# Modulation rows in four column groups, gate rows behind the first projection, and q/k/v transposes issued inside the following job

## The chip, the core and the metric

The kernel runs on one core of a Trainium2 chip. The metric is the device time in microseconds (us) of one execution. TensorE (PE) multiplies, its weight loads have a row of their own (PEld); VectorE (DVE), ScalarE (ACT) and GpSimd (POOL) do elementwise work; SyncE's queue (SP) issues most transfers.

## The reference, cut to what matters

Two layers. Each modulates the stream `u = h * (1 + scale) + shift`, projects it, and lets three mixers read it; attention needs all of q, k and v.

```
shift, scale, gate = split(silu(c) @ w_mod[l] + b_mod[l], 3)       # 1024 -> 3 x 1024, latent
shift_c, scale_c, gate_c = the same from c_ctx                      # context tokens
u_lat = h_lat * (1 + scale) + shift;  u_ctx = h_ctx * (1 + scale_c) + shift_c
p = u @ w_in[l]                                                     # q, k, v, gates, conv inputs
q = rope(rms_norm(q, q_gain)); k = rope(rms_norm(k, k_gain))        # 8 query heads, 2 kv heads, 64 wide
o = attention(q, [k_ctx; k_lat], [v_ctx; v_lat]); merge of three branches; @ w_out
h = layer_norm(alpha * h + gate * out)
```

1024 latent and 256 context tokens; in the last layer the context tokens give only k and v.

## The kernel before

Features lie on the partitions: a projection **job** computes 128 output features for all tokens T (1280 in layer 0, 1024 for most of layer 1) into one of two PSUM slots. Its weights are split by POOL into a high and a low part (`wh`, `wl`, lines 493 and 495), the input likewise (`Uh`, `Ul`), and for each of 8 blocks k of the contraction the job issues three products, `wh*Uh`, `wl*Uh`, `wh*Ul` (line 608). Job 0 of each layer is special: since `Uh` and `Ul` are still being made, it first does all products with `Uh`, waiting per block, and then all with `Ul` (line 613).

**Modulation.** `csilu` holds silu(c) and silu(c_ctx), 2 columns for each of 8 blocks. `mod_rows` (line 640) multiplies it with 512 columns of `w_mod` at a time: an output of 2 partitions x 512. Layer 0 takes the 2048 shift and scale columns from the tiles `wmA`, 8 tiles of 1 MB and four products each, and the 1024 gate columns from `wmB`, 8 tiles of 0.5 MB and two products each; layer 1 takes all six products of a block from `wmL`. DVE copies the rows out (`mod_row`, line 1163), PE transposes them into columns in pieces of 128 (`mod_cols`, line 648), and DVE adds the bias (`mod_col`, lines 1168 and 1173). Then `make_u` (ACT lines 891 and 895, DVE lines 1188 and 1193) makes `Uh` and `Ul` from blocks of h. In layer 0 these blocks are loaded in pairs into two buffers: SP's order is wmA, the first pair, the weights of jobs 0 and 1, all of wmB, and then the other three pairs, each block as soon as the one before it in its buffer was read (line 426). The rope tables land where wmB was, so their loads wait until the gate rows are done, and POOL's tables (line 515) wait for them. In layer 1 the rows of `wmL` are interleaved with the two LayerNorm statistics of layer 0's end (`stat`, line 633): block 0, the mean, blocks 1 to 4, the variance, blocks 5 to 7.

**q, k and v.** Jobs 0 to 5 are K, Q0, Q1, Q2, Q3 and V. After each, ACT copies the slot to one of two buffers `fc` (`evac`, line 912), PE transposes it to token-major form (line 626) in pieces of at most 4 x 128 tokens, alternating between two PSUM banks, and ACT copies each piece to one of two `raw` buffers (line 920) and squares it (line 934). DVE sums the squares (`mean_square`, 1208), POOL takes the power -0.5 (`rms`, 523), and DVE normalises, multiplies by the rope tables and adds (`normed`, lines 1215 to 1240). The normalised keys are transposed back (`to_keys`, operations KT0 and KT1), ACT copies them and DVE takes the low part (line 1247). V needs a copy and a low part on DVE (lines 956 and 1264). On DVE the order is K, Q0, Q1, KT0, KT1, Q2, Q3, V, each a mean square and a norm. Attention starts on PE with line 712, and before it all of these must be there.

PE's order in both layers is: job 0, job 1, K transposes, job 2, Q0 transposes, job 3, Q1 and KT0, job 4, KT1, Q2 and Q3, job 5, V, attention.

Of the kernel before, what the change touches and what calls it, by code (L numbers as in the profile page):

```python
# [17 lines left out]
F32 = mybir.dt.float32  # L18
F32R = mybir.dt.float32r
ACT = mybir.ActivationFunctionType  # L20
# [166 lines left out]
def build(nc, hT_in, cvec, wmod, w8, w4, vecs, gains, rope, ident_in, stack_in, outT):  # L187
    with ExitStack() as ctx:
# [11 lines left out]
        def at(name, shape, dt, offset):  # L200
            return nc.alloc_sbuf_tensor_at(name, shape, dt, offset=offset)
# [23 lines left out]
        modrow = [at("modrow0", [2, 3 * D], F32, rY), at("modrow1", [2, 3 * D], F32, rU + 5 * 12288)]  # L225
# [44 lines left out]
        csilu = small("csilu", [P, KD, 2])  # L270
# [96 lines left out]
        def jobs_qkv(l):  # L367

            return [TALL] + [TL[l]] * 4 + [TALL]
# [112 lines left out]
        def _(pool):  # L482
# [20 lines left out]

            nc.gpsimd.memset(ones[:], 1.0 / D).then_inc(s_ones, 1)
            nc.gpsimd.memset(mhalf[:], -0.5).then_inc(s_ones, 1)
            nc.gpsimd.memset(eps[:], LN_EPS).then_inc(s_ones, 1)
            pool.wait_ge(s_ones, 3)
# [85 lines left out]
        def _(pe):  # L593
# [27 lines left out]
            def transposes(l, op, srcs):  # L621

                for f, c, n in pieces(l, op):
# [20 lines left out]
            def mod_cols(l, first, n, at_col, turn):  # L644

                pe.wait_ge(s_modrow, turn)
                for m in range(first, first + n):
                    last = nc.tensor.transpose(PS[:, at_col + 2 * m:at_col + 2 * m + 2],
                                               modrow[l][0:2, m * P:(m + 1) * P], ident[0:2, 0:2])
                last.then_inc(s_modtr, 1)  # L650

            pe.wait_ge(s_csilu, 1)
            for k in range(KD):
                mod_rows(k, wmA, 0, 2 * D, s_wm[k], 16)
            mod_cols(0, 0, 2 * KD, 3072, 1)
            for k in range(KD):
                mod_rows(k, wmB, 2 * D, D, s_wmb, 16 * KD)

            for l in range(DEPTH):
# [5 lines left out]
                def qkv_job(n):  # L665
                    job((jl + n) // 2, n % 2, KD, jobs_qkv(l)[n], Uh, Ul,
                        (lambda k: pe.wait_ge(s_ufp, KD * l + k + 1)) if n == 0 else None,
                        (lambda k: pe.wait_ge(s_u, KD * l + k + 1)) if n == 0 else None)

                def to_tokens(f, n):  # L670
                    pe.wait_ge(s_fc, 6 * l + n + 1)
                    transposes(l, f, [fc[n % 2][:, t * P:(t + 1) * P] for t in range(jobs_qkv(l)[n] // P)])

                def to_keys(f, g):
                    pe.wait_ge(s_kd, l + 1)
                    transposes(l, f, [kd[:, t, g].rearrange("p a d -> p (a d)") for t in range(NTOK)])
# [180 lines left out]
                if nxt:  # L857
                    for p in range(2):
                        pe.wait_ge(sfree[p], (jl + NJ) // 2)
                    mod_rows(0, wmL, 0, 3 * D, s_wm[0], 32)  # L860
                pe.wait_ge(s_csum, 4 * l + 3)
                stat(l, O_OMEAN, e[4])
                if nxt:
                    for k in range(1, 5):
                        mod_rows(k, wmL, 0, 3 * D, s_wm[k], 32)
                pe.wait_ge(s_csum, 4 * l + 4)
                stat(l, O_OVAR, e[5])
                if nxt:
                    for k in range(5, KD):
                        mod_rows(k, wmL, 0, 3 * D, s_wm[k], 32)  # L870
                    mod_cols(l + 1, 0, 3 * KD, 0, 3)
# [3 lines left out]
        def _(act):  # L875
# [3 lines left out]
            fn(csilu[:], craw[:], ACT.Silu).then_inc(s_csilu, 1)  # L879
# [21 lines left out]
            for l in range(DEPTH):  # L901
# [45 lines left out]
                if l > 0:  # L947
                    act.wait_ge(s_hst, 16 * KD)
                k_hi(O_KT0, 0)
                evac(4)  # L950
                k_hi(O_KT1, 1)
                square(O_Q2)
                square(O_Q3)
                evac(5)
# [201 lines left out]
        def _(dve):  # L1156
# [4 lines left out]
            def mod_row(l, c0, n, turn):  # L1161
# [3 lines left out]
            def mod_col(l, first, n, at_col, turn):  # L1165
                dve.wait_ge(s_modtr, turn)
                cols = PS[:, at_col + 2 * first:at_col + 2 * (first + n)].rearrange("p (n w) -> p n w", w=2)
                last = tt(mod[:, l, first:first + n], cols,
                          vec[:, l, V_BM + first:V_BM + first + n].rearrange("p (n w) -> p n w", w=1)
                          .broadcast_to([P, n, 2]), ALU.add)  # L1170
                if first == 0:
                    st.done(last)
                    last = ts(mod[:, l, KD:2 * KD], mod[:, l, KD:2 * KD], 1.0, None, ALU.add)
                last.then_inc(s_mod, 1)

            mod_row(0, 0, 2 * D, 1)
            mod_col(0, 0, 2 * KD, 3072, 1)

# [17 lines left out]
            mod_row(0, 2 * D, D, 2)  # L1196
            mod_col(0, 2 * KD, KD, 3072, 2)

            for l in range(DEPTH):
# [305 lines left out]
                for j in range(KD):  # L1505
                    if l + 1 < DEPTH and j == KD // 2:
                        mod_row(l + 1, 0, 3 * D, 3)
                    tt(Z[:, j, :T], Z[:, j, :T], e[4][:, :T], ALU.mult).then_inc(s_norm, 1)
                if l + 1 < DEPTH:
                    mod_col(l + 1, 0, 3 * KD, 0, 3)  # L1510
                    make_u(l + 1, lambda j: X[:, j, :], lambda j: dve.wait_ge(s_hn, KD * l + j + 1))
# [69 lines left out]
```

## Time and profile before

| | us |
|---|---|
| median of 3 runs | 2991.51 |
| the three runs | 2988.11, 3004.97, 2991.51 |
| span of the profiled execution | 2990.4 |
| PE busy in it | 2783.8 (93%) |
| PEld busy | 2230.2 (75%) |
| DVE / POOL / ACT busy | 1472.9 / 876.1 / 819.5 |

The page gives no own time of the profiled execution beside its span; the median of the runs is 1.1 us above the span. PE is busy nearly everywhere. What it isn't lies in a few places, among them the first 75 us, the q/k/v stretch of either layer, and the passage from layer 0 to layer 1 at about 1600 to 1680 us.

### The profile page before, as it was taken

The numbers are of one execution on the slowest core, as the hardware profiler recorded it, in microseconds if no ns is written. First come the engines' busy times: TensorE is split into PE (matmuls) and PEld (weight loads), VectorE is DVE, ScalarE is ACT, GpSimd is POOL, SyncE is SP. The second block draws the span as 40 slices with busy tenths as digits, with TensorE's granted clock in tenths as the row PEclk, the third lists the DMA queues.
The fourth block names the chain that finished last, engine by engine and source line by source line (L and its number), as shares of the span: only waits on it lengthen the run. The fifth ranks groups of instructions, "written<-read, shape, count | busy, mean of one in ns | idle before, by whom it ended". The sixth has DMA issues, their size and how long they took to land.

```text
span 2990.4 us, 35900 instructions
## 1 busy us (share of the span) xinstructions
PE 2783.8 (93%) x13592; PEld 2230.2 (75%) x13592; DVE 1472.9 (49%) x1428; ACT 819.5 (27%) x1334; POOL 876.1 (29%) x818
## 2 busy tenths in 40 slices
PE   8889997999999999989999779999999999999994
PEld 3767776788888888878884557777888888877872
DVE  2577773216742168731225567775136323862135
ACT  2357673200001110120112447775100111012013
POOL 1610000223333233323232440000444434543340
PEclk9989997999999999999999889999999999999996
DMA  7100000011211113212233300000112111321221
GB/s 292 36 8 0 0 0 1 29 39 50 77 60 35 42 59 105 90 43 65 79 143 129 120 29 1 0 0 7 43 49 85 63 49 48 118 84 60 98 78 63
DMA packets 47033, 177.70 MB, mean 59 GB/s; under 512 B 5472, under 2 KB 5728, under 8 KB 44896
## 3 DMA queue, kind: packets, MB, share of 16 engines
q1 hardware_dynamic: 37728, 138.74, 13.6%
q10 hardware_dynamic: 9216, 37.75, 3.6%
q8 instruction: 59, 0.97, 0.1%
q14 instruction: 30, 0.25, 0.0%
HBM read 148.16 MB, written 28.31 MB: 59 GB/s over the span
## 4 chain that ended last, share of the span: by engine, by line
PE 79%; DVE 7%; ACT 6%; issue 5%; SPq 1%; POOL 1%; DMA 1%; DVEq 0%; ACTq 0%; POOLq 0%
PE PS L608 65%; PE PS L770 4%; PE PS L734 3%; PE PS L746 2%; DVE PTl L1313 1%; ACT Pr L978 1%; ACT Pr L982 1%; PE PS L640 1%; PE PS L757 1%; DVE nm L1286 1%; PE PS L712 1%; DVE e L1467 1%; DVE Ul L1489 1%; PE PS L633 1%; DMA wmB<-wmod 1%
## 5 line engine op out<-in xcount | busy, mean ns | idle before, releaser
L608 PE MATMUL PS<-Uh,wh 128*128 128x512 f32 x2816 | 773.6, 372 | 13.9 <-ACT Uh L895 12.3
L608 PE MATMUL PS<-Uh,wl 128*128 128x512 f32 x2816 | 769.7, 371 | 0.0
L608 PE MATMUL PS<-Ul,wh 128*128 128x512 f32 (+1 forms) x2728 | 744.7, 370 | 0.0
L493 POOL CAST wh<-wraw 128x512 fp32r<-128x512 f32 (+1 forms) x376 | 293.7, 781 | 1424.5 <-PE PS L608 963.6
L608 PEld LDWEIGHTS PS<-Uh,wh 128*128 128x128 f32 x2816 | 490.8, 189 | 113.1 <-issue 12.5
L608 PEld LDWEIGHTS PS<-Uh,wl 128*128 128x128 f32 x2816 | 490.9, 189 | 97.4
L608 PEld LDWEIGHTS PS<-Ul,wh 128*128 128x128 f32 x2728 | 474.5, 188 | 94.2
L495 POOL TENSOR_TENSOR wl<-wraw,wh 128x512 fp32r<-128x512 f32 (+1 forms) x376 | 510.0, 1356 | 30.1
L1372 DVE SCALAR_TENSOR_TENSOR cv<-hc,vec,cv x360 | 394.4, 1123 | 49.7 <-DVE cv L1372 38.0
L1054 ACT ACTIVATE e<-PS 128x1280 f32<-128x1280 f32 (+1 forms) x48 | 54.5, 1135 | 754.8 <-PE PS L608 754.7
L1313 DVE TENSOR_TENSOR PTl<-PS,PTh 128x512 fp32r<-128x512 f32 x328 | 211.1, 684 | 55.5 <-ACT PTh L996 48.1
L1286 DVE TENSOR_REDUCE nm<-PS 128x1 f32<-128x1280 f32 (+1 forms) x144 | 196.8, 1372 | 62.3 <-PE PS L734 53.5
L770 PE MATMUL PS<-ident,Pr 128*128 128x128 f32 x1312 | 187.5, 284 | 41.1 <-DVEq L1304 12.9
L996 ACT ACTIVATE PTh<-PS 128x512 fp32r<-128x512 f32 x328 | 183.6, 602 | 133.8 <-PE PS L770 133.3
L770 PEld LDWEIGHTS PS<-ident,Pr 128*128 128x128 f32 x1312 | 145.6, 143 | 77.4 <-DVE PTl L1313 33.6
L734 PE MATMUL PS<-kT,qTh 128*128 128x512 f32 (+1 forms) x400 | 167.3, 418 | 14.6 <-ACT Pr L978 7.7
L553 POOL COPY qd<-qo 128x512 f32 (+1 forms) x36 | 22.0, 616 | 536.9 <-PE PS L734 532.5
L734 PE MATMUL PS<-kT,qTl 128*128 128x512 f32 (+1 forms) x400 | 148.6, 372 | 0.0
L608 PE MATMUL PS<-Yh,wh 128*128 128x512 f32 (+1 forms) x480 | 133.0, 374 | 13.5 <-DVE Yl L1482 13.5
L982 ACT ACTIVATE Pr<-PS,nm 128x1024 f32<-128x1024 f32 x128 | 142.9, 1117 | 0.0
L1400 DVE SCALAR_TENSOR_TENSOR e<-PS,vec,e 128x1280 f32<-128x1280 f32 (+1 forms) x16 | 22.7, 1418 | 234.9 <-PE PS L608 234.9
L746 PE MATMUL PS<-PTh,Vt 128*128 128x512 f32 x328 | 137.2, 418 | 0.0
(135 smaller groups left out, 2525.2 us busy)
## 6 DMA issues: line engine op xcount, KB each, us to landing
wraw<-w SPq DMA_DIRECT2D x140, 512.0 KB, 3.5
wraw<-w SPq DMA_DIRECT2D x48, 256.0 KB, 2.7
wmL<-wmod SPq DMA_DIRECT2D x8, 1536.0 KB, 12.0
e<-hT_in SPq DMA_DIRECT2D x16, 640.0 KB, 4.7
accd<-e ACTq DMA_DIRECT2D x16, 640.0 KB, 3.2
e<-accd ACTq DMA_DIRECT2D x16, 640.0 KB, 4.0
wmA<-wmod SPq DMA_DIRECT2D x8, 1024.0 KB, 12.2
accd<-e ACTq DMA_DIRECT2D x16, 512.0 KB, 3.0
```

The source lines that it names most:

```text
L493: nc.gpsimd.tensor_copy(wh[par][:, s], wraw[par][:, s]).then_inc(whi[par], 1)
L495: nc.gpsimd.tensor_tensor(wl[par][:, s], wraw[par][:, s], wh[par][:, s].bitcast(F32), ALU.subtract).then_inc(wsplit[par], 1)
L608: last = mmul(PS[:, SLOT[par] + c:SLOT[par] + c + n], w[par][:, k * P:(k + 1) * P], x[:, k, c:c + n], start=(k == 0 and a == 0), stop=(k = ...
L734: last = mmul(PS[:, s0 + c:s0 + c + n], x[g][:, h * P:(h + 1) * P], kT[:, g, k0 * P + c:k0 * P + c + n], start=(a == 0), stop=(a == 1))
L746: last = mmul(PS[:, O0:O0 + 512], Vt[:, k0 + kt, g, :], x[b][:], start=(kt == 0 and a == 0), stop=(kt == nk - 1 and a == 1))
L770: last = nc.tensor.transpose(PS[:, PT0[par] + h * P:PT0[par] + (h + 1) * P], Pr[:, g, h, kt * P:(kt + 1) * P], ident[:])
L982: fn(Pr[:, g, h, c:c + 1024], PS[:, s0 + c:s0 + c + 1024], ACT.Exp, bias=nm[:, m:m + 1], accum_out=rs[:, g, 1, h:h + 1]).then_inc(s_exp, 1)
L996: fn(PTh[pt_buf(g, kt)][:], PS[:, PT0[par]:PT0[par] + 512], ACT.Copy).then_inc(pt_hi[par], 1)
L1054: fn(e[0][:, :T], slot(0, T), ACT.Sigmoid).then_inc(sfree[0], 1)
L1286: nc.vector.reduce_max(nm[:, m:m + 1], PS[:, s0:s0 + nk * P], AX_X, negate=True).then_inc(s_nm, 1)
L1313: tt(PTl[b][:], PS[:, PT0[par]:PT0[par] + 512], PTh[b][:].bitcast(F32), ALU.subtract).then_inc(pt_free[par], 1)
L1372: last = stt(cv[:, i + c_base, c0:c0 + n], hc[:, i + c_base, CPAD * who + c0 + tap:CPAD * who + c0 + tap + n], vec[:, l, bass.ds(i * CONF_ ...
```

## The change

Three things are changed.

1. `csilu` gets 32 columns for each block, 2 real ones and 30 zeros (a memset on POOL, for which ACT waits once at the start), and a product of `mod_rows` writes 32 partitions x 512, at partition 32q for the q-th 512 columns: four column groups of the array and one PSUM bank for shift and scale, two groups and another bank for the gate. The number of products stays 32 + 16 + 48. DVE's copy becomes 128 x 512 (64 x 512 for the gate), PE's transposes 4 of 128 partitions (4 of 64) in place of 16 (8) of 2 partitions, and the bias is added through a strided view.
2. In layer 0 the 16 gate products run behind job 0 and not ahead of it, and their 4 transposes inside job 2.
3. The K, Q0 and Q1 transposes run inside jobs 2, 3 and 4 (a piece ahead of some block k of the contraction), KT0 and KT1 inside job 5, and Q2, Q3 and V behind job 5. On ACT `evac(4)` comes ahead of KT0, and `evac(5)` ahead of the square of Q3. DVE, POOL and SP keep their order.

```diff
-            def mod_rows(k, w, col0, ncol, landed, n):
+            def mod_rows(k, w, parts, landed, n):
 
                 pe.wait_ge(landed, n)
-                for n in range(ncol // 512):
-                    last = mmul(PS[0:2, col0 + n * 512:col0 + (n + 1) * 512], csilu[:, k, :],
-                                w[k][:, n * 512:(n + 1) * 512], start=(k == 0), stop=(k == KD - 1))
+                for col0, ncol, bank in parts:
+                    for q in range(ncol // 512):
+                        last = mmul(PS[32 * q:32 * q + 32, bank:bank + 512], csilu[:, k, :],
+                                    w[k][:, col0 + q * 512:col0 + (q + 1) * 512], start=(k == 0), stop=(k == KD - 1))
                 last.then_inc(s_wmu, 1)
...
             for k in range(KD):
-                mod_rows(k, wmA, 0, 2 * D, s_wm[k], 16)
-            mod_cols(0, 0, 2 * KD, 3072, 1)
-            for k in range(KD):
-                mod_rows(k, wmB, 2 * D, D, s_wmb, 16 * KD)
+                mod_rows(k, wmA, [(0, 2 * D, 0)], s_wm[k], 16)
+            mod_cols(0, [(0, P, 3072)], 1)
...
+                def in_job2(k):
+                    if l == 0 and k == 1:
+                        mod_cols(0, [(1, 64, 3072)], 2)
+                    if l == 0 and k == 2:
+                        pe.wait_ge(s_mod, 2)
+                    if k in (3, 4, 6):
+                        to_tokens(O_K, 0, (3, 4, 6).index(k))
+
+                def in_job34(f, n):
+                    def hook(k):
+                        if k in (2, 3, 5):
+                            to_tokens(f, n, (2, 3, 5).index(k))
+                    return hook
+
+                def in_job5(k):
+                    if 1 <= k < 4:
+                        to_keys(O_KT0, 0, k - 1)
+                    if 4 <= k < 7:
+                        to_keys(O_KT1, 1, k - 4)
 
                 qkv_job(0)
                 if l == 0:
-                    pe.wait_ge(s_mod, 1)
-                    mod_cols(0, 2 * KD, KD, 3072, 2)
-                    pe.wait_ge(s_mod, 2)
+                    for k in range(KD):
+                        mod_rows(k, wmB, [(0, D, 3584)], s_wmb, 16 * KD)
                 qkv_job(1)
-                to_tokens(O_K, 0)
-                qkv_job(2)
-                to_tokens(O_Q0, 1)
-                qkv_job(3)
-                to_tokens(O_Q1, 2)
-                to_keys(O_KT0, 0)
-                qkv_job(4)
-                to_keys(O_KT1, 1)
+                qkv_job(2, in_job2)
+                qkv_job(3, in_job34(O_Q0, 1))
+                qkv_job(4, in_job34(O_Q1, 2))
+                qkv_job(5, in_job5)
                 to_tokens(O_Q2, 3)
                 to_tokens(O_Q3, 4)
-                qkv_job(5)
                 to_tokens(O_V, 5)
...
-                nc.vector.tensor_copy(modrow[l][:, c0:c0 + n], PS[0:2, c0:c0 + n]).then_inc(s_modrow, 1)
+                for part, rows, bank in parts:
+                    last = nc.vector.tensor_copy(modrow[l][0:rows, part, :], PS[0:rows, bank:bank + 512])
+                last.then_inc(s_modrow, 1)
```

At the kernel's start PE has this order before (`modrow` are the modulation rows; the first job's rows start with `Uh`):

```order
L640 MATMUL PS<-wmA_80,csilu 2x512 x4
L648 MATMUL PS<-ident,modrow_63 128x2 x16
L640 MATMUL PS<-wmB_81,csilu 2x512 x2
...
L640 MATMUL PS<-wmB_88,csilu 2x512 x2
L608 MATMUL PS<-Uh,wh_121 128x512 x2
```

And this one after:

```order
L644 MATMUL PS<-wmA_80,csilu 32x512 x4
L653 MATMUL PS<-ident,modrow_63 128x128 x4
L609 MATMUL PS<-Uh,wh_121 128x512 x2
...
L614 MATMUL PS<-Ul,wh_121 128x256
L644 MATMUL PS<-wmB_81,csilu 32x512 x2
...
L644 MATMUL PS<-wmB_88,csilu 32x512 x2
L609 MATMUL PS<-Uh,wh_122 128x512 x2
```

The gate rows have moved from ahead of job 0 (weights `wh_121`) to between it and job 1 (`wh_122`), and every product is 32 partitions high.

Around job 5 of layer 0 PE has this before (`kd` are the normalised keys, `fc_58` and `fc_57` the two feature copies, `qd` the first operand of attention):

```order
L608 MATMUL PS<-Ul,wh_121 128x256
L626 MATMUL PS<-ident,kd 128x128 x10
L626 MATMUL PS<-ident,fc_58 128x128 x10
L626 MATMUL PS<-ident,fc_57 128x128 x10
L608 MATMUL PS<-Uh,wh_122 128x512 x2
...
L626 MATMUL PS<-ident,fc_58 128x128 x10
L712 MATMUL PS<-ident,qd_108 128x128 x4
```

And this after:

```order
L609 MATMUL PS<-Ul,wh_122 128x256
L629 MATMUL PS<-ident,kd 128x128 x2
L609 MATMUL PS<-Uh,wh_122 128x512 x2
...
L609 MATMUL PS<-Ul,wh_122 128x256
L629 MATMUL PS<-ident,fc_58 128x128 x10
L629 MATMUL PS<-ident,fc_57 128x128 x10
L629 MATMUL PS<-ident,fc_58 128x128 x10
L732 MATMUL PS<-ident,qd_108 128x128 x4
```

The key transposes have moved into job 5, and those of Q2 and Q3 from ahead of job 5 to behind it, where only V's stood.

## Rows read from the trace of the kernel before

**Rows 1.** Stretches of time: stretch, length, busy us (instructions) per engine, PE clock, DMA, GB/s

```profile
30.00:35.00 5.00, 5.00 (x13) 0.97 (x12) 0.00 (x0) 0.00 (x0) 4.76 (x6) 1.00 1.03 415
40.00:45.00 5.00, 4.66 (x19) 1.34 (x19) 2.18 (x5) 3.71 (x4) 0.00 (x0) 0.70 0.19 50
```

**Rows 2.** Timeline, 8 to 78 us: start, us, engine, line, operation [idle before, releaser]

```profile
8.03 29.24 PE L640 MATMUL PS<-wmA,csilu 128*2 128x512 f32 x64 [8.03 <-DMA wmA<-wmod]
...
29.77 0.61 POOL L493 CAST wh<-wraw 128x512 fp32r<-128x512 f32 x1 [28.73 <-DMA wraw<-w]
...
37.31 2.28 DVE L1163 COPY modrow<-PS 2x2048 f32<-2x2048 f32 x1 [37.31 <-PE PS L640]
...
41.13 15.59 PE L640 MATMUL PS<-wmB,csilu 128*2 128x512 f32 x32 [0.34 <-DMA wmB<-wmod]
41.26 1.73 ACT L891 ACTIVATE e<-e,mod 128x1024 f32<-128x1024 f32 x2 [36.29 <-DVE mod L1173]
...
46.79 1.73 ACT L891 ACTIVATE e<-e,mod 128x1024 f32<-128x1024 f32 x2 [1.34 <-DMA e<-hT_in]
...
62.16 1.28 ACT L895 ACTIVATE Uh<-e 128x1280 fp32r<-128x1280 f32 x1 [1.13 <-DVE e L1188]
...
66.08 4.83 PE L613 MATMUL PS<-Ul,wh 128*128 128x512 f32 x24
...
71.35 2.94 POOL L515 TENSOR_TENSOR e<-cosT,gain 128x1280 f32<-128x1280 f32 x1 [33.93 <-DMA gain<-gains]
...
77.14 0.61 POOL L493 CAST wh<-wraw 128x512 fp32r<-128x512 f32 x1
```

**Rows 3.** Chain of waits, in order of time: start, us, what

```profile
71.75 14.29 PE PS L608 x72
...
145.79 13.78 PE PS L608 x72
...
1684.88 11.16 PE PS L608 x48
```

**Rows 4.** Timeline, q/k/v of layer 0, columns as in rows 2

```profile
140.52 1.07 PE L626 MATMUL PS<-ident,fc 128*128 128x128 f32 x8
...
161.06 2.44 DVE L1240 TENSOR_TENSOR qo<-qa,qb 128x1280 f32<-128x1280 f32 x1
...
164.52 2.15 DVE L1264 TENSOR_TENSOR Vt<-raw,Vt 128x1280 fp32r<-128x1280 f32 x1 [1.01 <-ACT Vt L956]
...
167.75 1.94 PE L712 MATMUL PS<-ident,qd 128*128 128x128 f32 x8 [4.98 <-POOL qd L553]
```

**Rows 5.** Timeline, from layer 0 to layer 1, columns as in rows 2

```profile
1598.24 5.31 PE L640 MATMUL PS<-wmL,csilu 128*2 128x512 f32 x12 [1.62 <-issue]
...
1600.10 1.78 DVE L1502 TENSOR_TENSOR e<-e,Z 128x1280 f32<-128x1280 f32 x1
...
1603.48 2.51 PE L633 MATMUL PS<-e,ones 128*128 128x512 f32 x6
...
1633.08 15.61 PE L640 MATMUL PS<-wmL,csilu 128*2 128x512 f32 x36
...
1642.04 5.70 DVE L1508 TENSOR_TENSOR Z<-Z,e 128x1280 f32<-128x1280 f32 x4
...
1648.73 3.35 DVE L1163 COPY modrow<-PS 2x3072 f32<-2x3072 f32 x1 [0.99 <-PE PS L640]
```

**Rows 6.** Timeline, job 0 and q/k/v of layer 1, columns as in rows 2

```profile
1662.38 1.40 PE L608 MATMUL PS<-Uh,wh 128*128 128x512 f32 x3 [8.22 <-ACT Uh L895]
...
1698.81 1.27 ACT L934 ACTIVATE sq<-raw 128x1280 f32<-128x1280 f32 x1
...
1763.40 1.22 DVE L1240 TENSOR_TENSOR qo<-qa,qb 128x1024 f32<-128x1024 f32 x1
...
1769.42 1.49 DVE L1264 TENSOR_TENSOR Vt<-raw,Vt 128x1280 fp32r<-128x1280 f32 x1 [4.80 <-ACT Vt L956]
...
1772.09 1.94 PE L712 MATMUL PS<-ident,qd 128*128 128x128 f32 x8 [4.43 <-POOL qd L553]
```

More of the change, by code:

```diff
@@ L269, in build @@
         craw = small("craw", [P, KD, 2])
-        csilu = small("csilu", [P, KD, 2])
+        csilu = small("csilu", [P, KD, 32])
         mod = small("mod", [P, DEPTH, 3 * KD, 2])
@@ L502, in split_merge @@
                         split(i * 4 + (jb // 2 + j), 1, W3)
+            nc.gpsimd.memset(csilu[:], 0.0).then_inc(s_ones, 1)
             nc.gpsimd.memset(ones[:], 1.0 / D).then_inc(s_ones, 1)
@@ L506, in _ @@
             nc.gpsimd.memset(eps[:], LN_EPS).then_inc(s_ones, 1)
[L507 removed]
+            pool.wait_ge(s_ones, 4)
             for l in range(DEPTH):
@@ L619, in piece_wait, with transposes @@
                     pe.wait_ge(t_free, f - 1)
-            def transposes(l, op, srcs):
-                for f, c, n in pieces(l, op):
+            def transposes(l, op, srcs, which=None):
+                for i, (f, c, n) in enumerate(pieces(l, op)):
+                    if which is not None and which != i:
+                        continue
                     piece_wait(f)
@@ L633, in stat, with mod_cols @@
                     mmul(tbank(f, n), ones[:], src[:, c:c + n], start=True, stop=True).then_inc(t_done, 1)
-            def mod_rows(k, w, col0, ncol, landed, n):
+            def mod_rows(k, w, parts, landed, n):
                 pe.wait_ge(landed, n)
-                for n in range(ncol // 512):
-                    last = mmul(PS[0:2, col0 + n * 512:col0 + (n + 1) * 512], csilu[:, k, :],
-                                w[k][:, n * 512:(n + 1) * 512], start=(k == 0), stop=(k == KD - 1))
+                for col0, ncol, bank in parts:
+                    for q in range(ncol // 512):
+                        last = mmul(PS[32 * q:32 * q + 32, bank:bank + 512], csilu[:, k, :],
+                                    w[k][:, col0 + q * 512:col0 + (q + 1) * 512], start=(k == 0), stop=(k == KD - 1))
                 last.then_inc(s_wmu, 1)
-            def mod_cols(l, first, n, at_col, turn):
+            def mod_cols(l, parts, turn):
                 pe.wait_ge(s_modrow, turn)
-                for m in range(first, first + n):
-                    last = nc.tensor.transpose(PS[:, at_col + 2 * m:at_col + 2 * m + 2],
-                                               modrow[l][0:2, m * P:(m + 1) * P], ident[0:2, 0:2])
+                for part, rows, at_col in parts:
+                    for m in range(4):
+                        last = nc.tensor.transpose(PS[:, at_col + m * rows:at_col + (m + 1) * rows],
+                                                   modrow[l][0:rows, part, m * P:(m + 1) * P], ident[0:rows, 0:rows])
                 last.then_inc(s_modtr, 1)
@@ L671, in to_tokens, with to_keys @@
+                def to_tokens(f, n, which=None):
                     pe.wait_ge(s_fc, 6 * l + n + 1)
-                    transposes(l, f, [fc[n % 2][:, t * P:(t + 1) * P] for t in range(jobs_qkv(l)[n] // P)])
-                def to_keys(f, g):
+                    transposes(l, f, [fc[n % 2][:, t * P:(t + 1) * P] for t in range(jobs_qkv(l)[n] // P)], which)
+                def to_keys(f, g, which=None):
                     pe.wait_ge(s_kd, l + 1)
-                    transposes(l, f, [kd[:, t, g].rearrange("p a d -> p (a d)") for t in range(NTOK)])
+                    transposes(l, f, [kd[:, t, g].rearrange("p a d -> p (a d)") for t in range(NTOK)], which)
@@ L878, in _ @@
             act.wait_ge(s_c, 64)
-            fn(csilu[:], craw[:], ACT.Silu).then_inc(s_csilu, 1)
+            act.wait_ge(s_ones, 4)
+            fn(csilu[:, :, 0:2], craw[:], ACT.Silu).then_inc(s_csilu, 1)
             def make_u(l, src):
@@ L1158, in _, with mod_row, mod_col @@
             tt, stt, ts = nc.vector.tensor_tensor, nc.vector.scalar_tensor_tensor, nc.vector.tensor_scalar
-            def mod_row(l, c0, n, turn):
+            def mod_row(l, parts, turn):
                 dve.wait_ge(s_wmu, KD * turn)
-                nc.vector.tensor_copy(modrow[l][:, c0:c0 + n], PS[0:2, c0:c0 + n]).then_inc(s_modrow, 1)
-            def mod_col(l, first, n, at_col, turn):
+                for part, rows, bank in parts:
+                    last = nc.vector.tensor_copy(modrow[l][0:rows, part, :], PS[0:rows, bank:bank + 512])
+                last.then_inc(s_modrow, 1)
+            def mod_col(l, parts, turn):
                 dve.wait_ge(s_modtr, turn)
[L1167 to L1173, printed above, removed]
+                for part, rows, at_col in parts:
+                    nq, first = rows // 32, 2 * KD * part
+                    cols = PS[:, at_col:at_col + 4 * rows].rearrange("p (m q w) -> p q m w", m=4, q=nq, w=32)
+                    last = tt(mod[:, l, first:first + 4 * nq].rearrange("p (q m) w -> p q m w", m=4),
+                              cols[:, :, :, 0:2],
+                              vec[:, l, V_BM + first:V_BM + first + 4 * nq].rearrange("p (q m w) -> p q m w", m=4, w=1)
+                              .broadcast_to([P, nq, 4, 2]), ALU.add)
+                    if part == 0:
+                        st.done(last)
+                        last = ts(mod[:, l, KD:2 * KD], mod[:, l, KD:2 * KD], 1.0, None, ALU.add)
                 last.then_inc(s_mod, 1)
-            mod_row(0, 0, 2 * D, 1)
-            mod_col(0, 0, 2 * KD, 3072, 1)
+            mod_row(0, [(0, P, 0)], 1)
+            mod_col(0, [(0, P, 3072)], 1)
             def make_u(l, src, landed):
```

34 lines of the change are left out of this document (18 added, 16 removed).

## The prediction

> **What bounds the kernel now.** I read the page first: PE is busy 93% of the span and its products are the chain nearly everywhere, so the three edits can only change stretches in which PE waits, or does work that they shorten. I then read the stretches by timeline and chain. There are four: the start up to job 1, q/k/v of layer 0, the passage to layer 1, and q/k/v of layer 1. In each the reader is to see which wait ends last.
>
> At the start the rows of wmA hold PE from 8.03 to 37.27 [rows 2]: 64 records of 0.43 us on average, two for each of 32 products, one behind the other. But the transfers are saturated too, 415 GB/s [rows 1], in the order in which SP issued them: the first job's weights are used at 29.77, and wmB lands at 41.13 [rows 2], though it was issued long before. Then `make_u` runs from 41.26, and its second pair starts only at 46.79, since its block was issued when the first was read (41.26 + 1.73 = 43.0) and took 3.8 us. A pair takes 5.6 us, and the last `Uh` ends at 63.44. PE does the gate rows meanwhile (41.13 to 56.72) and then job 0, and job 1 starts at 71.75 [rows 2, 3]. So the gate rows are free today: they lie under `make_u`.
>
> In q/k/v of layer 0 PE stands for some us between jobs, and from job 5's end at 159.57 to 167.75 ahead of attention [rows 3, 4]. There V's copy, transposes and low part (DVE, 164.52 to 166.67) come last; the norms of Q2 and Q3 had job 5 as cover and ended at 163.50 [rows 4]. In layer 1 V's low part is last again (1770.91), but DVE's norm of Q3 ended at 1764.62, with DVE idle for 4.8 us in between [rows 6].
>
> **The start.** With several column groups at work a block of wmA takes less time on PE than its 1 MB takes to land (1.05 MB at 0.42 MB/us is 2.5 us; PE needs 29.24 / 8 = 3.66 us today). The transfers set the end: from the first weights at 29.77 I go back by 0.52 MB of weights and 1.31 MB of the first pair, 4.4 us, so the last wmA tile is there at about 25.4. Then products 0.9 to 2.2, copy 0.6 (2.28 for 2048 columns [rows 2], now 512), transposes 0.6, bias 0.4, latencies: the modulation stands at about 29 in place of 41.2. That looks like 12 us. But the second pair lies in SP's queue behind wmB, which lands at 41.1 as before. It lands at about 42.5, so of 12 us the chain of `make_u` keeps 46.79 - 42.5 = 4.3. The last `Uh` ends at 59.1. Job 0 follows it: one block, 1.2 us at full clock or 2.3 at half (the first in layer 1 took 1.40 for three of its six products after a pause [rows 6]), then the `Ul` products, 4.83 [rows 2]. PE will have stood long before, and the granted clock falls after pauses (0.70 of full in 40 to 45 us [rows 1], between levels of 1.2 and 2.4 GHz). I take 66.5, between 65.1 and 71. Now the gate rows, which were free, stand in the path: 16 products, 15.59 us one by one [rows 2]. Of two column groups I expect half: 7. Job 1 starts at 73.6, **1.9 us later than before**. The rope loads wait for the gate rows: POOL's tables started 6.3 us behind the last `Ul` (63.44 + 1.5, against 71.35) and need 5.8, and the first half of job 2's weights 2 more [rows 2], so 73.5 + 14.1, against job 1's end at 73.6 + 14.3 [rows 3]. No stall, with no margin; a miss costs 1 or 2 us.
>
> The copy width, the csilu memset (0.3 us on idle POOL) and DVE's wait for the gate transposes in job 2 (nothing is queued behind it until the first squares) I put at nothing.
>
> **The trace against the Trainium skill.** The rows show that two columns of weights stream no faster than 128, and that nothing ran side by side; no row shows column groups. The Trainium skill (TensorE: Matmul & The Clock Gate, Part 3: Packing small matmuls) reports 2.38 times for three column tiles of 32 with 512 columns. It also says that matmuls start in program order; with two records for each fp32 product on one group, this would allow one product per 0.43 us, not four at once. By that the gate rows are 6.9 us too and the rest of my sum stands, since transfers bound wmA. The page on DMA: Bandwidth & Descriptors (Queues, rings and completion order) has descriptors consumed in ring order, which agrees with 29.77 against 41.13 above; no run here shows the contrary.
>
> **q/k/v of layer 0.** Removed are PE's pauses at the edges of jobs 2 to 5: from job 1's end at 86.04 [rows 3] to attention are 81.7 us, in which four jobs take 13.8 to 13.9 each, and 8.2 are the end, so 18 go into the edges. In their place stand the transposes, 50 of 0.13 us (1.07 for 8 [rows 4]), in the jobs, 6.5, and 4 gate transposes, 0.5. Job 5 then ends 62.5 us behind job 1 in place of 73.5: 11 gained. But behind it now stands all of Q2, Q3 and V. From the first Q2 transpose to the end of Q3's norm are 140.52 to 163.50, 23.0 us [rows 4], of which about 0.5 was ACT being busy with KT1, so 22.5; then V's low part, which is behind it on DVE, 1.5 to 2.15 (1.6), and 1.1 from there to PE (166.67 to 167.75). That makes 25.2 in place of 8.2: 17 lost. **Sum +6.0.** The K squares come about 9 us later, which moves POOL's tables and the norms; they still end just ahead of job 5's end, and job 4's weights about 1 us ahead of its start. This is tight: +0 to +3, and if ACT's `evac(5)` ahead of Q3 costs its 1.25 once more, +1.
>
> **The passage.** Block 0's six products take 5.31 and hold the mean's product until 1603.48, though its sum was ready at 1600.10 + 1.78 = 1601.9 [rows 5]. Shorter by half or more they end before it: -1.5. The variance waits for DVE. Blocks 5 to 7, 15.6 us, end at 1648.7, and DVE, done with four Z at 1647.74, waits 1.0 for them, then copies 3.35 [rows 5]. Half the products, even at half clock to begin with, end before that, and two copies of 512 take 1.3: -1.0 - 2.05. **Sum -4.5**, all on the chain into `make_u`.
>
> **q/k/v of layer 1.** The DVE chain decides. K's squares start 2.8 us behind job 1's end (1684.88 + 11.16 = 1696.04) [rows 3, 6]; with its last piece ahead of block 6 of job 2 (6 x 1.39 + 1.3 of transposes and copies) it is 10.2, so 7.5 later. From there DVE and POOL went without waiting for PE up to the norm of Q3, ended 1764.62; now 1772.1. V's low part, 1.5, and 1.2 to PE [rows 6]: 1774.8 against 1772.09. **+2.8** (-1 to +6, for POOL and DVE slow each other when they meet: a copy of 1280 on DVE takes 1.49 alone, 2.15 and more then).
>
> **Sum.** +1.9 + 6.0 - 4.5 + 2.8 = +6.2. On the span of 2990.4 that is 2996.6; the median stood 1.1 above it, so 2997.7, rounded 2998.
>
> **Rivals.**
> - **The column groups do not overlap**, the case that ends slower. For it: nothing in the trace shows them working at once. Then wmA ends at 37.3 as before and only the copy is shorter (-1.5); job 0 ends at 69.0, the gate rows take 15.6 in the path, and job 1 starts at 84.7, +12.9. With +6.0, with -2.0 at the passage (the copy alone) and +2.8: **+19.7, 3011.** It decides where two groups take over some 12 us for the gate rows.
> - **The second pair overtakes wmB.** Then it lands 3.8 us after its issue at 31, job 0 ends at about 58.5, and job 1 starts at 65.6: -6.1 + 6.0 - 4.5 + 2.8 = **-1.8, 2990.** Against it: the order of landing above.
> - **The norm chain is no limit**, so that attention starts as soon behind job 5 as in layer 0 before, 8.2 us. Layer 0 then gains 11, layer 1 I put at 11.5, its edges costing as much: 1.9 - 11 - 4.5 - 11.5 = **-25, 2966.** This is what hiding transposes would bring if PE's pauses were all. Against it: Q2's and Q3's norms take the same 23 us wherever they start, and only job 5 covered them.
> - **A cold clock through job 0 and the gate rows**: +4.5 for `Ul` and +3 to 5 for the rows, **3006.**
>
> **How the numbers follow.** My forecast 0.60, no overlap 0.18, overtaking 0.09, cold clock 0.08, no limit 0.05. The forecast's own range is 2990 to 3005. The range from 2988 to 3012 takes in all but the fourth and some of no overlap. A measurement of this kernel can tell about 0.5%, 15 us, from no change. Faster by more than that is the -25 case, 0.05; slower (over 3006.5) is no overlap and part of the cold clock, 0.21; the same 0.74.
>
> **What the profile after would show.** Right: the first `Uh` at about 31, a pause on PE until about 43 behind two blocks, the second pair at 42.5; gate rows of about 7 us between jobs 0 and 1; no pauses inside jobs 2 to 5; 25 us between job 5 and line 732's transposes in layer 0 and some 22 in layer 1, with DVE busy; the mean's product at about 2 us after the last sum; DVE's modulation copy at once behind the fourth Z. Wrong: gate rows of 15 us, a second pair before 40, or attention within 15 us of job 5.

## The result, and the profile after

The changed kernel takes 3014.32 us (median of 20 runs, 2997.37 to 3017.21), the kernel before 3002.81 (20 runs, 2988.11 to 3008.1): a ratio of **1.0033, 95% interval 1.0019 to 1.0048**. The change costs about 10 us (5.7 to 14.4). The profiled execution of the changed kernel has a span of 3009.2, the one of before 2990.4, and of these 18.8 us only some 11 are the change's. The rest is told under the fourth experiment. A difference of a third of a per cent is small, so what the change does is read from the stages of the traces, and the ratios only say whether they add up.

The start of the changed kernel, by timeline (start, us, engine, line, operation [idle before, releaser]):

```profile
25.24 1.06 PE L644 MATMUL PS<-wmA,csilu 128*32 128x512 f32 x8 [0.74 <-DMA wmA<-wmod]
26.38 0.69 DVE L1185 COPY modrow<-PS 128x512 f32<-128x512 f32 x1 [26.38 <-PE PS L644]
...
28.25 1.73 ACT L912 ACTIVATE e<-e,mod 128x1024 f32<-128x1024 f32 x2 [23.30 <-DVE mod L1199]
...
42.53 1.73 ACT L912 ACTIVATE e<-e,mod 128x1024 f32<-128x1024 f32 x2 [10.09 <-DMA e<-hT_in]
...
58.22 1.27 ACT L916 ACTIVATE Uh<-e 128x1280 fp32r<-128x1280 f32 x1 [1.11 <-DVE e L1214]
...
60.81 4.83 PE L614 MATMUL PS<-Ul,wh 128*128 128x512 f32 x24
...
65.57 7.06 PE L644 MATMUL PS<-wmB,csilu 128*32 128x512 f32 x32
...
72.56 0.85 PE L609 MATMUL PS<-Uh,wh 128*128 128x512 f32 x3
```

Read against [rows 2]: the column groups work at once. The last four products of wmA take 1.06 us where four took 29.24 / 8 = 3.66, and the 16 gate products 7.06 where they took 15.59. The modulation stands at 28.25 in place of 41.26. Of these 13 us the second pair of h gives back all but 4.3 (42.53 against 46.79), since ACT waits 10.09 us for it, and the gate rows take back more than the rest: job 1 starts at 72.56, 0.8 later than before.

The stretch ahead of attention in layer 0, by the same view:

```profile
137.89 3.53 POOL L524 TENSOR_TENSOR rstd<-ms,mhalf 128x20 f32<-128x20 f32 x1 [3.90 <-DVE ms L1235]
...
148.36 0.74 PE L609 MATMUL PS<-Ul,wh 128*128 128x512 f32 x3
...
148.94 1.04 PE L629 MATMUL PS<-ident,fc 128*128 128x128 f32 x8
...
151.94 1.51 ACT L941 ACTIVATE raw<-PS 128x512 f32<-128x512 f32 x3 [4.61 <-DVEq L1274]
...
152.10 1.49 DVE L1273 TENSOR_TENSOR kT<-raw,kT 64x1280 fp32r<-64x1280 f32 x1 [0.24 <-DVE kT L1273]
...
178.00 1.94 PE L732 MATMUL PS<-ident,qd 128*128 128x128 f32 x8 [14.39 <-POOL qd L554]
```

Job 5 ends at about 148.9, where before it ended at 159.57 [rows 3]. The pauses between jobs are gone. But attention starts at 178.00 against 167.75 [rows 4], and PE stands 14.39 us ahead of it in place of 4.98. From the last K transposes on, the chain up to there has nothing of PE in it but two short groups of transposes (0.45 us at 152.59, 0.70 at 156.71); it goes over POOL and DVE:

```profile
99.05 0.23 PE PS L629 x2
99.31 0.39 ACT raw L941
...
99.72 1.28 ACT sq L955
...
101.03 1.50 DVE ss L1234
...
106.31 7.11 POOL e L516 x2
...
137.89 3.54 POOL rstd L524
...
175.52 1.42 DVE Vt L1290
...
178.00 1.95 PE PS L732 x8
```

Later the passage to layer 1 (timeline):

```profile
1619.64 1.78 DVE L1528 TENSOR_TENSOR e<-e,Z 128x1280 f32<-128x1280 f32 x1
1621.53 2.51 PE L636 MATMUL PS<-e,ones 128*128 128x512 f32 x6 [1.85 <-DVEq L1529]
...
1666.11 1.27 DVE L1185 COPY modrow<-PS 128x512 f32<-128x512 f32 x2
...
1674.51 1.73 ACT L912 ACTIVATE e<-X,mod 128x1024 f32<-128x1024 f32 x2
...
1698.69 1.24 ACT L933 ACTIVATE fc<-PS 128x1280 f32<-128x1280 f32 x1 [6.20 <-PE PS L614]
...
1719.73 1.27 ACT L955 ACTIVATE sq<-raw 128x1280 f32<-128x1280 f32 x1
...
1791.63 1.94 PE L732 MATMUL PS<-ident,qd 128*128 128x128 f32 x8 [12.49 <-POOL qd L554]
```

The mean's product waits for DVE now and no longer stands behind block 0's rows [rows 5], and the copy of the rows takes 1.27, not 3.35. From line 1528 (1619.64) to `make_u` (1674.51) are 54.87 us. Attention in layer 1 starts 117.12 us behind `make_u`, and PE waits 12.49 us for it where it waited 4.43 [rows 6]. The row at 1698.69 is the end of job 0 in this layer; the account of the prediction comes back to it.

### The profile page after: what moved, and what is told of

Same layout as the page of the kernel before. It is cut to its first block, busy times and chain, and to the rows that moved or that the text cites. A ratio compares the mean times of both kernels' runs of the same rounds, so it can differ in the third digit from the quotient of the medians.

```text
span 3009.2 us, 35856 instructions
## 1 busy us (share of the span) xinstructions
PE 2743.8 (91%) x13560; PEld 2224.3 (74%) x13560; DVE 1474.1 (49%) x1430; ACT 820.3 (27%) x1334; POOL 883.0 (29%) x819
## 4 chain that ended last, share of the span: by engine, by line
PE 75%; DVE 9%; issue 6%; ACT 6%; POOL 2%; DMA 2%; DVEq 0%; SPq 0%; ACTq 0%; POOLq 0%
PE PS L609 62%; PE PS L790 4%; PE PS L754 3%; PE PS L766 2%; DVE PTl L1339 1%; ACT Pr L999 1%; ACT Pr L1003 1%; PE PS L777 1%; DVE nm L1312 1%; DMA e<-hT_in 1%; PE PS L732 1%; DVE e L1493 1%; DVE Ul L1515 1%; POOL wl L495 1%; POOL rstd L524 1%
## 5 line engine op out<-in xcount | busy, mean ns | idle before, releaser
L754 PE MATMUL PS<-kT,qTh 128*128 128x512 f32 (+1 forms) x400 | 165.3, 414 | 15.6 <-ACT Pr L999 8.5
```

Of the source, the lines that this page charges most:

```text
L754: last = mmul(PS[:, s0 + c:s0 + c + n], x[g][:, h * P:(h + 1) * P], kT[:, g, k0 * P + c:k0 * P + c + n], start=(a == 0), stop=(a == 1))
```

## The experiments

All ratios are to the kernel before, on the same chip. Diffs are against the changed kernel, and in them a minus is what the changed kernel has.

### The column groups alone

The gate rows go back ahead of job 0, and all transposes (those of the gate rows too, between jobs 0 and 1) and `evac` back to their old places.

```diff
+            for k in range(KD):
+                mod_rows(k, wmB, [(0, D, 3584)], s_wmb, 16 * KD)
...
-                qkv_job(2, in_job2)
-                qkv_job(3, in_job34(O_Q0, 1))
...
+                to_tokens(O_K, 0)
+                qkv_job(2)
+                to_tokens(O_Q0, 1)
+                qkv_job(3)
```

> The column groups alone: modulation rows as in the changed kernel, but the gate rows ahead of job 0 and all q/k/v transposes between the jobs as before. My theory (groups help, the two moves hurt): the gate rows run at about 41 to 48 us under the making of u, job 0 ends at about 65.6 and job 1 starts at about 66.5, 5 us earlier than before; the passage to layer 1 is 4 us shorter; in all 9 us faster than before, ratio 0.997. Rival (the groups are worth nothing because transfers or DVE set these stretches anyway): within 2 us of before.

Measured: 2993.65 us, ratio **0.9973 (0.9954 to 0.9992)**. Job 1 starts at 66.47, 5.3 earlier than before, and attention in layer 0 at 164.09, 3.7 earlier. The first part of the change gains 8 us (2 to 14). By stages it is 3.7 up to attention in layer 0, 4.8 in the passage (54.32 against 59.10) and 2.0 in q/k/v of layer 1 (110.94 from `make_u` to attention, against 112.89). What loses must be in the other two.

### The moved transposes alone

The narrow rows and the old place of the gate rows, with the third part of the change kept.

```diff
-                        last = mmul(PS[32 * q:32 * q + 32, bank:bank + 512], csilu[:, k, :],
+                    last = mmul(PS[0:2, col0 + n * 512:col0 + (n + 1) * 512], csilu[:, k, :],
...
+                    mod_cols(0, 2 * KD, KD, 3072, 2)
```

> The moved q/k/v transposes alone (part 3 of the change) on the kernel before. My theory: +6 to +9 us in q/k/v of layer 0 and +3 to +5 us in that of layer 1, with 23 to 26 us between job 5 and attention in layer 0; in all 10 to 13 us slower, ratio 1.004. Rival (the loss lies in the gate rows behind job 0 and not here): within 3 us of before.

Measured: 3015.78 us, ratio **1.0039 (1.0026 to 1.0053)**, about 12 us lost. Its start is that of before (job 1 at 71.71 against 71.75), and attention starts at 175.94, 8.2 later. In layer 1 attention stands 118.62 us behind `make_u` where before it stood 112.89, 5.7 later, which is more than the 3 to 5 expected. The whole loss of the third part is in these two stretches, with nothing of the modulation in it; the passage is 1.5 shorter in this profile.

### The gate rows ahead of job 0

```diff
+            for k in range(KD):
+                mod_rows(k, wmB, [(0, D, 3584)], s_wmb, 16 * KD)
...
-                if l == 0:
-                    for k in range(KD):
-                        mod_rows(k, wmB, [(0, D, 3584)], s_wmb, 16 * KD)
```

> The changed kernel with part 2 undone: the gate rows run ahead of job 0 again, their transposes still inside job 2. My theory: job 1 starts at about 65.6 us in place of 72.6, everything behind it 7 us earlier, so 7 us faster than the changed kernel and some 3 us slower than before. Rival (the rope tables' loads, which wait for the gate rows, or the clock set job 1's start): no more than 2 us faster than the changed kernel.

Measured: 3004.12 us, ratio **0.9998 (0.9982 to 1.0013)**, about 10 us below the changed kernel (the two intervals leave 2 to 20). Job 1 starts at 64.93 in place of 72.56, and attention in layer 0 at 169.85 in place of 178.00. By the trace it is thus about 8 us, close to the 7 expected. The second part of the change is a loss by itself. With the gate rows behind job 0, PE waits 9.34 us under `make_u` (to 45.62). Here they start when wmB lands, run from 41.10 to 49.86, and job 0 has made up for it by its last block, for which PE waits 0.30 us at 58.82. Behind job 0 PE has no such wait.

### The kernel before once more

> The kernel before once more, for a second profile of it. The changed kernel's products in the loops of layer 0 took 1.2% longer each than in the first profile of before (682.2 against 674.4 us for the same 3528), in code that the change does not touch. If that varies from execution to execution, this profile may show either figure, and its span either about 2990 or about 3003; if it belongs to the change, this profile shows 674 us again and 2990.

Measured: 3000.42 us, ratio 0.9996 (0.9976 to 1.0016). The longest piece in each chain (start, us, what), of before, of before once more, of the changed kernel and of the last experiment below:

```profile
580.31 674.37 PE PS L608 x3528
```

```profile
577.37 686.12 PE PS L608 x3528
```

```profile
590.27 682.21 PE PS L609 x3528
```

```profile
572.65 674.38 PE PS L609 x3528
```

The same instructions in the same program take 674.37 in one execution and 686.12 in another. So the 7.84 us by which the changed kernel's profile is longer here are not the change's: 18.8 - 7.8 leaves 11.0, inside the 5.7 to 14.4 of the ratio. Whether this stretch is also the main reason why runs of before lie between 2988 and 3008 us is not shown. The second profile of before spans 2994.7, only 4.3 more than the first, though it lost 11.75 us here: attention in layer 0 up to this stretch took it 407.7 us in place of 412.6 (169.67 to 577.37, against 167.75 to 580.31), and other parts vary by a us or two. The expectation named a span of about 2990 or about 3003, and neither came.

### The h pairs issued ahead of wmB

In the changed kernel's SP order four tiles of wmB follow the second pair of h, and four the third.

```diff
-                            for k in range(KD):
-                                sp.dma_start(wmB[k][:], wmod[0, k][:, 2 * D:]).then_inc(s_wmb, 16)
...
+                        if j in (3, 5):
+                            for k in range(2 * (j - 3), 2 * (j - 3) + 4):
+                                sp.dma_start(wmB[k][:], wmod[0, k][:, 2 * D:]).then_inc(s_wmb, 16)
```

> The changed kernel with one change in SP's queue: the second and third pair of blocks of h are issued ahead of the first and second half of wmB. My theory (the second pair waits for its place behind wmB in the transfers, not for the modulation): it lands at about 34 us in place of 42.5, the last Uh ends at about 51, job 0 at about 58, the gate rows stand behind it with their tiles landed, and job 1 starts at about 65 in place of 72.6; 7 us faster than the changed kernel. Rival (blocks of h would land no sooner, or job 0 is held by the clock): under 2 us.

Measured: 3012.39 us, ratio **1.0026 (1.0008 to 1.0044)**, which can't be told from the changed kernel. The 7 us did not come. The timeline shows why:

```profile
35.58 1.73 ACT L913 ACTIVATE e<-e,mod 128x1024 f32<-128x1024 f32 x2 [1.53 <-DMA e<-hT_in]
...
46.23 1.73 ACT L913 ACTIVATE e<-e,mod 128x1024 f32<-128x1024 f32 x2 [3.44 <-DMA e<-hT_in]
...
54.38 1.73 ACT L913 ACTIVATE e<-e,mod 128x1024 f32<-128x1024 f32 x2 [3.96 <-DMA e<-hT_in]
56.14 2.43 ACT L917 ACTIVATE Uh<-e 128x1280 fp32r<-128x1280 f32 x2
...
61.90 5.15 PE L615 MATMUL PS<-Ul,wh 128*128 128x512 f32 x24
66.98 7.06 PE L645 MATMUL PS<-wmB,csilu 128*32 128x512 f32 x32
...
73.97 0.84 PE L610 MATMUL PS<-Uh,wh 128*128 128x512 f32 x3
```

The second pair is used at 35.58 in place of 42.53, 7 us earlier, as intended. Then the third stands behind four tiles of wmB and the fourth behind the other four. The last block of `Uh` is ready only 0.9 us earlier (56.14 + 2.43 = 58.57, against 58.22 + 1.27 = 59.49), and PE gives that back and more. It had stood for 4.13 us ahead of the last two blocks, its granted clock was 0.50 from 57.5 to 61.9 us (1.2 GHz), and it took both blocks one behind the other at that pace: six products take 2.50 us where the changed kernel's last six took 1.43 at 1.00. Job 1 starts at 73.97, 1.4 later. So the rival's second half came, job 0 held by the clock. This supports the order of landing that the prediction used: the second pair, no longer behind wmB, came at once, and the third, behind 2 MB of it, came 8.9 us after its issue at 37.34. It also shows that the queue was not one pair's problem: the bytes were only moved.

### The Q2 and Q3 transposes inside job 5

```diff
-                    if 1 <= k < 4:
-                        to_keys(O_KT0, 0, k - 1)
-                    if 4 <= k < 7:
-                        to_keys(O_KT1, 1, k - 4)
+                    if k < 3:
+                        to_keys(O_KT0, 0, k)
+                    if 3 <= k < 6:
+                        to_keys(O_KT1, 1, k - 3)
+                    if k == 6:
+                        to_tokens(O_Q2, 3)
+                    if k == 7:
+                        to_tokens(O_Q3, 4)
...
-                to_tokens(O_Q2, 3)
-                to_tokens(O_Q3, 4)
```

> The changed kernel with the transposes of Q2 and Q3 moved from behind job 5 to its blocks 6 and 7, behind those of the keys (and ACT's copy of V behind their squares). Theory A (the chain of norms on DVE and POOL, 7 to 9 us late since K's transposes came late, is what attention waits for): Q2's and Q3's copies find no free buffer before the keys' low parts are done, and attention starts only 0 to 4 us earlier in either layer. Theory B (only the place of Q2 and Q3 behind job 5 costs): attention starts some 10 to 15 us earlier in layer 0.

Measured: 3010.1 us, ratio 1.0017 (0.9994 to 1.004), against 1.0033 the same within the intervals. Attention in layer 0 starts at 179.43 (178.00), in layer 1 at 1791.41 (1791.63), and PE waits 14.38 us ahead of the first (14.39). 0.8 of the 1.4 us by which layer 0 is later are the start's (job 1 at 73.39, not 72.56). Theory B asked for 10 to 15 us earlier. That PE does Q2 and Q3 late is not the reason: offered earlier, they find the buffers of `raw` still taken by the keys and DVE still at the norm of Q1, and Q2's power came at 157.76 (156.56 in the changed kernel).

### Everything one job earlier

Column groups, gate rows ahead of job 0, K transposes in job 1, Q0 in job 2, Q1 in job 3, KT0 in job 4, and KT1, Q2 and Q3 in job 5. ACT's order follows, and POOL takes the power of K ahead of the split of job 3's weights.

```diff
-                def in_job2(k):
+                def in_job1(k):
...
+                    if k in (2, 3, 4):
+                        to_tokens(O_K, 0, k - 2)
...
+                def in_job4(k):
+                    if k in (3, 4, 5):
+                        to_keys(O_KT0, 0, k - 3)
...
+                    if k < 3:
+                        to_keys(O_KT1, 1, k)
+                    if k == 3:
+                        to_tokens(O_Q2, 3, 0)
+                        to_tokens(O_Q2, 3, 1)
...
+                qkv_job(1, in_job1)
+                qkv_job(2, in_job23(O_Q0, 1))
+                qkv_job(3, in_job23(O_Q1, 2))
+                qkv_job(4, in_job4)
```

> A version from what the runs so far show: column groups; gate rows ahead of job 0; K's transposes inside job 1, Q0's inside job 2, Q1's inside job 3, the first keys' inside job 4, the second keys', Q2's and Q3's inside job 5; POOL's power for K ahead of its split of job 3's weights. My theory (the chain of norms must start early, and must not stand behind job 5): job 1 starts at about 65, attention in layer 0 some 12 to 16 us earlier than before, the passage 4 us shorter, attention in layer 1 another 7 to 10 us earlier; in all 22 to 28 us faster than before, ratio 0.991 to 0.993. Rival (POOL's splits and tables take over as the limit when K comes earlier): no more than the 9 us of the column groups alone.

Measured: 2982.22 us (6 runs), ratio **0.9935 (0.991 to 0.9959)**. It beats both kernels, by about 20 us and 29 us, as the ratios have it, and stays just short of the 22 to 28 expected against before. By timeline:

```profile
74.38 1.27 ACT L964 ACTIVATE sq<-raw 128x1280 f32<-128x1280 f32 x1
...
143.34 4.71 POOL L524 TENSOR_TENSOR rstd<-ms,mhalf 128x20 f32<-128x20 f32 x1 [1.04 <-DVE ms L1244]
...
157.85 1.48 DVE L1299 TENSOR_TENSOR Vt<-raw,Vt 128x1280 fp32r<-128x1280 f32 x1
...
160.41 1.94 PE L741 MATMUL PS<-ident,qd 128*128 128x128 f32 x8 [13.90 <-POOL qd L554]
```

The squares of K come at 74.38 (99.72 in the changed kernel, of which 7.0 are the start's, 65.56 against 72.56), and attention at 160.41 in place of 178.00. That is 7.3 us ahead of before, where 12 to 16 were expected. The passage is 4.2 shorter, as expected, and q/k/v of layer 1 3.6 (109.28 against 112.89), where 7 to 10 were expected. Against the column groups alone, the early transposes are worth 3.7 us in layer 0 (160.41 against 164.09) and 1.7 in layer 1.

Why not more? The K chain is no longer the limit. DVE stands for 6.31 us ahead of the second keys' low part, and for 3.10 and 2.87 ahead of the mean squares of Q2 and Q3, whose squares (135.68 and 140.25) wait for PE: their transposes stand ahead of blocks 3 to 6 of job 5. From Q3's squares on, the chain is two norms and V's low part on DVE, and PE waits 13.90 us for it. So the same hidden transposes gain or lose according to the job that they are hidden in, and here the next ones to move are those of Q2 and Q3. The rival named POOL. It does delay Q0's and Q1's powers (DVE waits 7.34 and 6.77 us for them, where 3.65 is the usual), but the gain of about 20 us is more than the 9 that the rival allowed.

## Why the prediction was right or wrong

**The absolute time was low by the base.** 3014.3 lies above the range's end of 3012. The forecast shift was +6.2, and the measured one is about +10 (5.7 to 14.4). Between 2997.7 and 3014.3 lie 16.6 us, and 11.3 of them are the base: the three runs of before had their median at 2991.5, twenty at 3002.8. The term of the sum that was mis-sized most is therefore the one taken as given. The shown runs (2988 to 3005) already spread over 17 us, more than half the width of my range, and I gave that spread no room in it. The measured ratio on the base that I used gives 3001.4, inside the range. The other 5 us are in the shift, in the two q/k/v stretches, as told below.

**The start: right, with job 1 1 us early.** The modulation stood at 28.25 (forecast about 29), the second pair was used at 42.53 (42.5), the last `Uh` ended at 59.49 (59.1), and the gate rows took 7.06 (7). Job 0 ended at 65.6, not 66.5. The start cost 0.8, not 1.9. The rival without overlap falls with the 7.06, the one of the overtaking pair with the 42.53.

That the cold clock did not hurt was partly luck. The granted clock was 0.50 from 40 to 50 us and 0.51 up to 55, with PE standing from 36.3 to 45.6, and it was 1.00 from 55 on, before the last two blocks, `Ul` and the gate rows. In the run with the h pairs ahead it was still 0.50 at 61.9.

Two readings of mine were off and cost little. The 64 records take 29.24 / 64 = 0.46 us on average; the 0.43 is their pace from 11.8 us on, and the first ones came at half of it. And the gate rows weren't quite free before: with them ahead, `Ul` started 2.64 us behind the last `Uh` (66.08 against 63.44), in the changed kernel 1.32 (60.81 against 59.49).

I did not weigh the obvious alternative to this part, column groups with the gate rows left ahead of job 0. The third experiment shows what it was worth: job 1 7.6 us earlier, about 10 by the ratios. The idle 10.09 us of ACT ahead of the second pair were in my own forecast, and PE's wait under them is where the rows overlap `make_u`.

What I concluded from the Trainium skill's statement on program order (TensorE: Matmul & The Clock Gate, Part 2: What happens when you issue a matmul) doesn't hold. I read it as one product for each 0.43 us at best. For the pairs of the gate rows this is met, 7.06 / 16 = 0.44 each. But four products took 1.06 us at a granted clock of 1.00, 0.27 each, so starting in order does not forbid four at once:

```profile
25.20:26.40 1.20, 1.06 (x8) 0.16 (x8) 0.03 (x1) 0.00 (x0) 0.00 (x0) 1.00 1.01 418
65.60:72.60 7.00, 7.00 (x34) 1.79 (x33) 0.00 (x0) 1.24 (x1) 0.00 (x0) 1.00 0.00 0
```

These are stretches of the changed kernel: stretch, length, busy us (instructions) of PE, PEld, DVE, ACT and POOL, PE clock, DMA share, GB/s. One product alone took 0.87 at the same clock (18 in 15.61 us, at 1633.08 [rows 5]), a pair in two groups takes 7.06 / 8 = 0.88, and four in four groups 1.06: 2.0 and 3.3 times. The Trainium skill (same page, Part 3: Packing small matmuls) has 2.38 times for three, which lies between the two.

**q/k/v of layer 0: the reason was right, the working was not.** Jobs 2 to 5 ended 62.1 us behind job 1 (86.76 to 148.9, forecast 62.5). The tail is 29.1, not 25.2, so the stretch costs 9.5 us and not 6.0. The step that failed is "they still end just ahead of job 5's end", they being the norms ahead of Q2's. POOL's powers of -0.5, one for each norm, show it, first before and then after:

```profile
92.05 3.54 POOL L523 TENSOR_TENSOR rstd<-ms,mhalf 128x20 f32<-128x20 f32 x1 [2.00 <-DVE ms L1209]
...
112.98 3.54 POOL L523 TENSOR_TENSOR rstd<-ms,mhalf 128x20 f32<-128x20 f32 x1 [3.04 <-DVE ms L1209]
...
126.05 3.53 POOL L523 TENSOR_TENSOR rstd<-ms,mhalf 128x20 f32<-128x20 f32 x1 [0.53 <-DVE ms L1209]
```

```profile
102.80 3.54 POOL L524 TENSOR_TENSOR rstd<-ms,mhalf 128x20 f32<-128x20 f32 x1 [10.35 <-DVE ms L1235]
...
123.75 3.54 POOL L524 TENSOR_TENSOR rstd<-ms,mhalf 128x20 f32<-128x20 f32 x1 [3.03 <-DVE ms L1235]
```

K comes 10.75 late, Q0 10.77, Q1 11.84 (137.89 above against 126.05), and attention 10.25. From K's power to Q1's are 34.0 us before and 35.1 after: this part of the chain is nearly rigid, and was so before. DVE has K's norm in hand for 15.6 us of it in either kernel, with POOL at its tables and splits (one step takes 4.22 us, where it takes 1.48 in Q2's norm). What slack there was came behind Q1's norm, when DVE stood 4.99 us for the second keys, and it is used up. The norm of Q1 and KT1 end 4.7 us behind job 5 (at 153.6), ACT finds no free `raw` until 151.94, and the tail grows by 3.0 there and by about 1 in the norms. The forecast had +0 to +3 for this and left it out of the sum; it was 3.9. The sixth experiment confirms it, since earlier Q2 and Q3 change nothing, and the last one does by the other way, since there DVE waits for Q2 and Q3 and no longer for K. No run moves the K transposes alone, so their own share is read from the chain and not isolated.

**q/k/v of layer 1: right in kind, too small by half.** The chain of waits reads (before, then after):

```profile
1701.89 3.53 POOL rstd L523
...
1735.31 3.54 POOL rstd L523
```

```profile
1722.82 3.53 POOL rstd L524
...
1756.24 3.54 POOL rstd L524
```

From K's power to Q1's are 33.42 us both times. The two profiles differ here by +4.2 (117.12 against 112.89), but this comparison flatters the change. Job 0 of this layer ended 25.7 us behind `make_u` before (1684.92 - 1659.20, clock 0.81 from 1672 to 1680) and 24.2 after (1698.69 - 1674.51, clock 1.00 from 1687 to 1695). Nine profiles of eight programs have either 24.2 (before once more, the changed kernel and the sixth experiment) or 25.7 to 25.9, so this 1.5 varies from execution to execution:

```profile
1684.92 1.24 ACT L912 ACTIVATE fc<-PS 128x1280 f32<-128x1280 f32 x1 [7.74 <-PE PS L613]
```

Compared like with like the stretch costs 5.7: 117.12 against the 111.40 of before once more, or the second experiment's 118.62 against 112.89. The forecast was 7.5 late at K's squares less 4.8 of DVE's idle time ahead of V. The first is right, 7.1 (9.9 behind job 1's end where it was 2.8; my working, 6 x 1.39 + 1.3, gives 9.6 and not the 10.2 that I wrote). The second is right too, since V's low part follows Q3's norm without a gap now (DVE, 1788.96). The term that is missing is the chain between them: from K's squares to the end of Q3's norm it takes 69.3 us where it took 65.8, 3.5 more. 1.5 of it lie in Q1's norm and 2.0 behind it, where DVE waits 2.04 for Q3's squares and then meets POOL at its splits (a step of Q3's norm takes 2.28, where it took 1.23).

**The passage: right.** -4.2 against -4.5: line 1528 to `make_u` takes 54.87 where before it took 59.10 (1659.20 - 1600.10). Before once more has 59.06, the column groups alone 54.32. The second experiment, which has no column groups, has 57.59, so some 1.5 of the 4.2 may have another cause, which stays open.

**The sum.** +0.8 + 9.5 - 4.2 + 4.2 = +10.3 between the two profiles, and +11.8 with the 5.7 for layer 1. Both agree with the measured shift of about 10 (5.7 to 14.4). So the mechanism and the sign of each stage were right, and three sizes were not: the base (11.3 us), the tail of layer 0 (3.9 in place of 0) and the norm chain of layer 1 (3.5 in place of 0). The rival without a norm limit, -25, falls for this change, and for the last experiment too: PE still waits 13.90 us ahead of attention there, for two norms.

## What to carry to other kernels

Work hidden inside another job is late by as much of that job as stands ahead of it. Where a chain on other engines hangs on it, the lateness arrives at the end less the slack of the chain (here 10.8 us at K's squares and 10.3 at attention), and the idle time on PE that it removes comes back in one piece ahead of the consumer. So find the first link of the consumer's chain (here the K transposes) and move that earlier: the pauses go as well. Then look for the limit again, since it moves (here to Q2 and Q3). Before a range is given, put the spread of the shown runs into it. And before two profiles are compared stage by stage, take a second one of the same kernel: here a stage of it moved by 1.5 us and a stretch by 11.8 with nothing changed.

## What the runs showed of the hardware that was not expected

- Four fp32 products of 32 columns in four column groups take 1.06 us and two take 0.88, where one alone takes 0.87, all at a granted clock of 1.00.
- Where transfers set the pace of these rows the granted clock was 0.67 in 16 to 20 us and 0.58 in 20 to 25, part of it at 1.2 GHz in place of 2.4, and one block took up to 1.93 us in place of 1.06. PE had been busy for 2.30 of the 4 us and 3.67 of the 5, with no pause above 1.43. For all but the last block it cost nothing, as the next was 2.5 us away. The last took 1.06 in the changed kernel's profile, but 1.90 to 1.94 in the third, fifth and sixth experiments, and there the modulation stood at 29.2 to 29.9 and not at 28.25. The first two blocks took 1.93 and 1.94 as well, with a granted clock of 1.00 in the record (8 to 12 us), so the record doesn't show what slowed those.
- The stretch of 3528 records of products takes one of three times in nine profiles: 674.37 and 674.38 (before, the last experiment), 682.21 twice (the changed kernel, the third), and 686.12 to 686.15 (before once more, the first, second, fifth and sixth). The granted clock was 1.00 in all nine. The long stretch of layer 1, 2352 records, takes 546.58 in all nine. In 50 us one execution has 264 records of products and another 259, in the same program. What sets it isn't known. The first of these lines is of before (800 to 850 us), the second of before once more:

```profile
800.00:850.00 50.00, 50.00 (x264) 42.83 (x263) 39.00 (x42) 3.70 (x3) 15.71 (x17) 1.00 0.19 63
```

```profile
800.00:850.00 50.00, 50.00 (x259) 42.39 (x258) 38.08 (x42) 2.48 (x2) 14.08 (x16) 1.00 0.19 63
```
